# A projection in two sweeps: queries and gate of the retention computed chunk by chunk

## The reference, cut to what matters

```python
h  = rmsnorm(x, g_norm_mix) * (1.0 + sc1) + sh1          # [2048, 1024]
hc = rmsnorm(ctx, g_norm_mix) * (1.0 + csc1) + csh1      # [256, 1024]
cq, ckv, kr, rq, rk, rv, rg = split(h @ w_in, (256, 128, 32, 512, 512, 512, 512))   # the same for hc
q_a, k_a, v_a = mla_qkv(cq, ckv, kr, ...)                # rmsnorm, @ w_uq, @ w_ukv, 2-D rope
q, k = rope_2d(rq), rope_2d(rk * 64 ** -0.5)             # 8 heads of 64; gate = rg
# per direction (decay gamma_h), per chunk n of 128 tokens:
s       = (q_n @ k_n.T) * decay_in
u_n     = (k_n * zeta).T @ v_n
r_{n+1} = decay_chunk * r_n + u_n                        # starts from the context's state
y_n     = s @ v_n + (q_n * xi) @ r_n
# out: y normed per head, * g_ret, * silu(rg); concatenated with attention; @ w_o
```

## Time and profile before

| | us |
|---|---|
| median of 3 runs (lowest, highest) | 3234.02 (3233.12, 3239.76) |
| the profiled execution | 3241.32 |
| its span in the trace | 3239.5 |
| `modulation` | 0 to 124.6 |
| `project` | 124.6 to 897.8 |
| `retention` | 897.8 to 1103.9 |
| `attention`, `mix_out`, `experts` and final output | 1103.9 to 3239.5 |

### The profile page before, as it was taken

One profiled execution on the slowest core, in us unless ns is written; L12 is line 12 of the kernel. 1 busy time (PEld: TensorE's weight loads), 2 busy tenths in 40 slices (PEclk: granted clock), 3 DMA queues, 4 the chain that ended last, 5 costly groups with the idle time before them and its releaser, 6 DMA issues. The chain is left out here.

```text
span 3239.5 us, 55402 instructions
## 1 busy us (share of the span) xinstructions
PE 2990.5 (92%) x20325; PEld 2205.0 (68%) x20325; DVE 2014.4 (62%) x2973; ACT 1381.0 (43%) x2069; POOL 353.2 (11%) x385
## 2 busy tenths in 40 slices
PE   6799999999978699999999998899399999999997
PEld 1355555555578667666666665787398989899996
DVE  1133333333357599989899998445766666666766
ACT  0133333333222377677677765211244444444444
POOL 0011111111145200000000000221001111010102
PEclk9899999999977699999999999999599999999998
DMA  8511111111132301110111000533467676666768
GB/s 313 176 65 64 64 60 61 61 64 64 52 111 78 82 3 34 37 25 14 35 27 25 23 6 12 179 135 113 137 205 209 206 222 208 201 203 211 212 202 312
DMA packets 255042, 365.51 MB, mean 113 GB/s; under 512 B 36469, under 2 KB 170616, under 8 KB 253177
## 3 DMA queue, kind: packets, MB, share of 16 engines
q1 hardware_dynamic: 245336, 327.97, 31.5%
q0 software_dynamic: 9504, 34.61, 4.5%
HBM read 280.70 MB, written 81.83 MB: 112 GB/s over the span
## 5 line engine op out<-in xcount | busy, mean ns | idle before, releaser
L479 PE MATMUL bank<-w_in_sb,h_T 128*128 128x512 f32 (+1 forms) x1440 | 609.9, 578 | 2.1 <-DVE h_T L628 2.1
L1784 PE MATMUL ebank<-gathered_T,w_gate_up 128*128 128x256 f32 x4608 | 561.2, 284 | 21.8 <-issue 16.4
L1784 PEld LDWEIGHTS ebank<-gathered_T,w_gate_up 128*128 128x128 f32 x4608 | 556.7, 193 | 25.6 <-issue 20.7
L479 PEld LDWEIGHTS bank<-w_in_sb,h_T 128*128 128x128 f32 x1440 | 270.4, 191 | 299.4 <-issue 299.1
L1062 PE MATMUL abank<-head_qT,head_kT 96*128 96x512 f32 x1728 | 414.7, 400 | 23.2 <-DVE head_qT L1171 17.0
L1062 PEld LDWEIGHTS abank<-head_qT,head_kT 96*128 96x128 f32 x1728 | 326.3, 192 | 104.6 <-issue 29.6
L1142 ACT ACTIVATE scores<-scores 128x1536 f32<-128x1536 f32 x192 | 274.3, 1476 | 232.8 <-DVE scores L1201 232.8
L1201 DVE TENSOR_TENSOR scores<-scores,abank 128x1536 f32<-128x1536 f32 x192 | 322.7, 1748 | 44.9 <-PE abank L1082 44.8
L1137 ACT ACTIVATE scores<-abank 128x512 f32<-128x512 f32 x576 | 325.7, 602 | 42.5 <-PE abank L1062 17.1
L1092 PE MATMUL abank<-scores,head_v 128*64 128x256 f32 x2304 | 291.0, 388 | 1.2 <-ACT scores L1142 1.2
L1798 PE MATMUL ebank<-w_down,hidden_T 128*128 128x512 f32 x1152 | 282.0, 400 | 2.9 <-DVE w_down L2016 2.8
(11 more groups left out here) (266 smaller groups left out, 3291.8 us busy)
## 6 DMA issues: line engine op xcount, KB each, us to landing
w_gate_up_whole<-in_w_exp_gate SPq DMA_DIRECT2D x48, 1024.0 KB, 5.7
w_gate_up_whole<-in_w_exp_up SPq DMA_DIRECT2D x48, 1024.0 KB, 9.0
w_down_whole<-in_w_exp_down SPq DMA_DIRECT2D x192, 256.0 KB, 6.0
ada_w<-in_w_ada SPq DMA_DIRECT2D x12, 2048.0 KB
scratch_ret<-ret_rows SPq DMA_DIRECT2D x72, 256.0 KB, 2.5
x_tile<-in_x_all SPq DMA_DIRECT2D x18, 512.0 KB
w_in_sb<-in_w_in SPq DMA_DIRECT2D x4, 2048.0 KB, 18.2
chunk_qk<-scratch_ret SPq DMA_DIRECT2D x16, 512.0 KB
```

What stands on the lines that cost most here:

```text
L479: m = pe.matmul(banks[bank][:, 0:n], hT[u][:, k, :], w_in[:, k, lo:lo + n], start=(k == 0), stop=(k == KD - 1))
L1784: x = pe.matmul(banks[f % 3][:, j * CAP:(j + 1) * CAP], w_gu[c][:, wp, j, k, o:o + P], xsT[:, xp, k, :], start=(k == 0 and n == 0), stop=( ...
```

## The change

The projection's w_in is split into a rounded part and a rest, and so is h_T; the products take three fp32r matmuls per k-tile. The first sweep, `project`, computes only the latent, rk and rv. It stores the modulated h_T of each tile, and the state of each chunk, to DRAM. The attention's queries are left out for the context's two tiles. The products of a tile's turn are interleaved anew: two, transposes of the next x, transposes of the latent, the third product. h's rest is taken on VectorE at the end of its turn and waits for the store of h, since it overwrites it. The weights for rq and rg (4 MB) are loaded meanwhile.

The second sweep, `retention`, loads h_T, rk, rv and the states. At its start it splits the weights for rq and rg in 16 pieces. Per chunk TensorE makes both products of the next chunk back to back, then the scores, output transposes, transposes of the next chunk, outputs and the decayed transposes. VectorE ropes rq, decays the scores and after that computes the gate; the rest of h closes its turn. The scores and the transposed q_xi keep one buffer instead of two and share banks 4 and 5.

`modulation` gets three ScalarE copies and three VectorE subtractions that split w_in.

```diff
@@ modulation
+            for part, c in enumerate(IN_PARTS):                                   # ACT, after the decays
+                act.wait_ge(w_loaded[1 + part], 16)
+                act.activation(weights["in"][:, 0, :, c], weights["in_whole"][:, 1, :, c], ACT.Copy).then_inc(s_w_in, 1)
...
+                if 5 <= n < 8:                                                      # DVE
+                    c = IN_PARTS[n - 5]
+                    dve.wait_ge(s_w_in, n - 4)
+                    dve.tensor_tensor(weights["in"][:, 1, :, c], ..., ALU.subtract).then_inc(w_rest, 1)
@@ project, SP
+                store(t, "ret_k", rk[:, :], scratch["rk"][at, :], "rk_stored")
+                if ahead:
+                    store(t + 1, "hT", hT_whole[1 - u][:, 1, :, :], scratch["h"][bass.ds(row + P, P)], "h_stored")
...
+                store(t, "u_back", st[u][:, :], scratch["state"][at, :], "state_stored")
@@ project, TensorE
+            def z(t, u, bank, lo, n):
                 for k in range(KD):
+                    for i, (hp, wp) in enumerate(((0, 0), (0, 1), (1, 0))):
+                        m = pe.matmul(banks[bank][:, 0:n], hT[u][:, hp, k, :], w_in[:, wp, k, lo:lo + n],
+                                      start=(k == 0 and i == 0), stop=(k == KD - 1 and i == 2))
...
+                sg["h_rest"].wait(pe, t)
+                z(t, u, 0, 0, LAT)
+                z(t, u, 1, LAT, RW)
+                if ahead:
+                    xT(pe, t + 1, 1 - u)
                 sg["kr_lat"].wait(pe, t)
...
+                z(t, u, 3, LAT + RW, RW)
                 sg["latT"].wait(pe, t)
+                if queries:
...
-                z(u, 0, LAT + 2 * RW, RW)
-                z(u, 3, LAT + 3 * RW, RW)
@@ project, VectorE
+            def rest(t, u):
+                sg["h_stored"].wait(dve, t)
+                for g in range(2):
+                    k = slice(4 * g, 4 * g + 4)
+                    sg["h_rounded"].wait(dve, t, g + 1)
+                    dve.tensor_tensor(hT[u][:, 1, k, :], hT_whole[u][:, 1, k, :], hT[u][:, 0, k, :].bitcast(F32), ALU.subtract).then_inc(sg["h_rest"].sem, 1)
...
+                if ahead:
+                    x_norm(t + 1, 1 - u)
+                if not (isinstance(t, int) and t == 0):
+                    advance_state(t - 1, 1 - u)
...                                     # latent normed, rope of rk
+                if ahead:
+                    modulate(t + 1, 1 - u)
...                                     # latent_T scaled
+                if ahead:
+                    rest(t + 1, 1 - u)
@@ retention, TensorE
             def turn(r, u, first, ahead):
-                if ahead >= 1:
-                    scores(r + 1)
-                outputs(r, u)
-                if ahead >= 2:
-                    transposes(r + 2, u)
+                if ahead:
+                    z_query(r + 1, 1 - u)           # waits h_rest(r + 1), ret_q(r)
+                    z_gate(r + 1, 1 - u)            # waits gate(r)
+                scores(r)
                 if not first:
                     out_transposes(r - 1)
+                if ahead:
+                    transposes(r + 1, 1 - u)
+                outputs(r, u)
+                if ahead:
+                    decayed_transposes(r + 1)
@@ retention, VectorE
+            def turn(r, u, first, ahead):
+                if not first:
+                    out_rows(r - 1)
+                if ahead:
+                    rope_q(r + 1, 1 - u)
+                if ahead:
+                    next_carry(r + 1, 1 - u)
+                decay_scores(r)
+                if ahead:
+                    gate_rows(r + 1)
+                if ahead == 2:
+                    rest_h(r + 2, u)
@@ retention, ScalarE
+            def turn(r, u, first, ahead):
+                evacuate_kq(r)
+                if not first:
+                    square(r - 1)
+                evacuate_qx(r)
+                if ahead:
+                    gate_exp(r + 1)
                 if not first:
                     store(r - 1)
+                if ahead == 2:
+                    round_h(r + 2, u)
@@ retention, GpSimd
+                if not first:
+                    power_of(r - 1)
+                pool.tensor_tensor(gg[:, :], gate[:, :], gret[:, :], ALU.mult).then_inc(sg["gate_gain"].sem, 1)
+                if ahead:
+                    q_xi(r + 1)
```

More of the change, by code:

```diff
@@ L469, in xT @@
             m.then_inc(sg["xT_psum"].sem, 1)
-            sg["k_rows"].wait(pe, t - 1)
+            if not (isinstance(t, int) and t < 2):
+                sg["k_rows"].wait(pe, t - 2)
             for k in range(4):
@@ L544, in x_stats, with round_h, turn @@
                 act.activation(xst[:, 1:2], xst[:, 1:2], ACT.Exp, scale=-0.5).then_inc(sg["x_rstd"].sem, 1)
-            def turn(t, u, ahead):
+            def round_h(t, u):
+                sg["z_psum"].wait(act, t - 2)
+                for g in range(2):
+                    k = slice(4 * g, 4 * g + 4)
+                    sg["hT"].wait(act, t, 2 * g + 2)
+                    act.activation(hT[u][:, 0, k, :], hT_whole[u][:, 1, k, :], ACT.Copy).then_inc(sg["h_rounded"].sem, 1)
+            def turn(t, u, ahead, queries):
+                if ahead:
+                    x_stats(t + 1, 1 - u)
                 sg["z_psum"].wait(act, t, 1)
@@ L590, in _, with turn @@
         def _(pool):
-            def turn(t, u, ahead):
-                sg["q_rows"].wait(pool, t)
+            def turn(t, u, ahead, queries):
+                sg["ret_k"].wait(pool, t)
+                sg["u_psum"].wait(pool, t - 1)
+                for w in range(2):
+                    pool.tensor_tensor(kz[:, :, w, :], halves(rk[:, :]), last(perm["zeta"][:, w * H:(w + 1) * H], 64), ALU.mult).then_inc(sg["k_zeta"].sem, 1)
+                if not queries:
+                    return
+                n = t - TC
                 tables.wait(pool, t, u)
+                sg["q_rows"].wait(pool, n)
                 x = q_sb[:, :, NOPE:]
@@ L756, in _ @@
+            top = (T - 1) * P
+            load_h(top, 0)
+            load_back(P, 0)
+            sp.dma_start(back[1][b, :], scratch["state"][64:128, :]).then_inc(context_loaded, 16)
+            load_k(top, 0)
+            load_v(top, 0)
+            load_h(top - P, 1)
+            load_k(top - P, 1)
+            load_v(top - P, 1)
             sp.dma_start(gret[:, :], ins["g_ret"].partition_broadcast(P)).then_inc(gret_loaded, 16)
[L757 to L759 removed]
@@ L801, in _, with z @@
+            q_xi(0)
             loop(pool, turn)
+            power_of(TM - 1)
         @block.tensor
         def _(pe):
+            def z(r, u, bank, part, first):
+                for k in range(KD):
+                    if first:
+                        pe.wait_ge(w_rest, part * KD + k + 1)
+                    for i, (hp, wp) in enumerate(((0, w_hi), (0, w_lo), (1, w_hi))):
+                        m = pe.matmul(banks[bank][:, :], hT[u][:, hp, k, :], wp[:, k, part * RW:(part + 1) * RW],
+                                      start=(k == 0 and i == 0), stop=(k == KD - 1 and i == 2))
+                m.then_inc(sg["z_psum"].sem, 1)
@@ L805, in transposes, with z_query, z_gate @@
+            def z_query(r, u, first=False):
+                sg["h_rest"].wait(pe, r)
+                sg["ret_q"].wait(pe, r - 1)
+                z(r, u, 0, 0, first)
+            def z_gate(r, u, first=False):
+                sg["gate"].wait(pe, r - 1)
+                z(r, u, 1, 1, first)
             def transposes(r, u):
-                kq_loaded.wait(pe, r, u)
+                kb_loaded.wait(pe, r, u)
                 sg["chunk_kqT"].wait(pe, r - 1)
-                for b, which in ((0, 1), (1, 0)):
+                sg["ret_q"].wait(pe, r)
+                for bank, x in ((2, rk[u]), (3, rq)):
@@ L927, in turn, with out_rows @@
+            def out_rows(r):
                 sg["y_psum"].wait(dve, r)
```

536 lines of the change are left out of this document (307 added, 229 removed).

## The result

The changed kernel takes 3059.93 us (median of 4 runs, 3048.09 to 3068.14), the kernel before 3235.74 in 4 runs on the same chip: a ratio of 0.9453, with an interval of 0.9419 to 0.9486. The forecast was 3070 with a range of 3040 to 3140, and faster. The profiled execution of the changed kernel took 3068.14 us, with a span of 3066.3.

A forecast was written before the change was run, and what follows sets the result against it. TensorE alone was taken to bound the projection, while the retention ran at a mean clock of 0.72. First sweep -295.4 us and second +131.0 gave -164.4, so 3076.9 profiled and 3070 as median, range 3040 to 3140.

The forecast's parts named there:

- The product: Both sweeps: 24 fp32r matmuls of 512 columns take 5.55 us instead of 6.87 in plain f32.
- Rival E: Both sweeps: fp32r products as dear as f32 records, 408 us more, 3478; chance 0.01.
- The latent tile: First sweep: 25.0 us for each of 16 latent tiles, set by the chain through latent_T; bounds 23.9 and 28.
- collision: First sweep: modulation sums on VectorE beside GpSimd's k_zeta cost 1.32 us instead of 0.69; one or two hit.
- The context tiles: First sweep: 21.7 us for each of two tiles without queries, set by the store of h, above TensorE's 20.5.
- The chunk: Second sweep: 19.7 us a chunk, a loop closing through VectorE's rest of h; bounds 18.6 (TensorE) and 25.
- The fill: Start of the second sweep: loading h, rounding, splitting weights, rope and q_xi; first turn starts at 23.8 us.
- The end: End of the second sweep: last out_rows, decay, outputs, transposes, copy and barrier take 19.0 us.
- The price of the gate in front: Second sweep: with the gate before the decay, outputs wait until 18.3 and a chunk costs 4 us more.
- rival A: Second sweep keeps falling to the lower clock: 25.1 us a chunk, 81 us more, 3150; chance 0.13.
- B: First sweep: late h store or VectorE collisions make the turn 27.5 us instead of 25.0, 3110; chance 0.18.
- C: Fewer collisions: 24.0 us a turn in the first sweep, 18.8 in the second, 3041; chance 0.09.

The follow-up runs named there:

- late_latent: Changed kernel plus one VectorE row sum of 0.69 us just before it scales latent_T in the first sweep; 3076.87 us, one run.
- rest_first: Changed kernel with h's rest taken before the gate on VectorE in the second sweep, and that h rounded earlier on ScalarE; 3042.27 us, ratio 0.9382.
- no_reciprocal: Changed kernel with the gate's reciprocal left out in the second sweep; 3041.23 us, one run.
- gate_first: Changed kernel with VectorE computing the next chunk's gate before it decays the scores in the second sweep; 3173.76 us, ratio 0.9793.
- gate_first_busy: gate_first plus 14 fp32r products of constant operands on TensorE before the outputs of each chunk, result unread; 3120.99 us, one run.
- the two comparisons: Changed kernel against the kernel before, run twice: 3059.93 us, ratio 0.9453; again, unaltered, 3052.96 us, ratio 0.9424.

## Why the prediction was right, point by point

**What bounds the kernel, and where.** Right for both sweeps: in the steady stretches the only recorded waits of TensorE are those named.

**The product.** 5.55 us was taken from the output stage's 24 matmuls. Measured in the second sweep: (757.13 - 745.95)/2 = 5.59. What follows latent_T took 6.96 (357.81 to 364.77) for a forecast of 6.95. Rival E is out.

**The latent tile.** 25.0 predicted, 24.33 measured (389.2/16, with the shorter last one; 24.39 without it). The mechanism was right, late_latent shows it, and a term was mis-sized. The prediction had latent_T ready 18.1 us after the start of product 0; in the tile shown it was 17.4 (340.28 to 357.68). The steps one by one: 5.25 to z_latent (5.1), 5.8 to the last roped row (5.94), 2.1 for the rope (2.0), 3.2 for the modulation (353.43 to 356.63) where 2.74 and a collision of 0.9 to 1.0 were taken, 1.05 for the scaling (1.04). The collision cost 0.46, since just one of the two sums was hit for long; the other 0.3 are tenths added at handovers, which were in the durations already. The same tenths are in the 17.3 at which TensorE was said to want latent_T. The third product starts at 11.4 to 11.5 and takes 5.55, which gives 17.0, and only this agrees with the prediction's sum of 23.96 (17.0 + 6.95). So the chain is late by some 0.4, where the prediction took 0.8.

What the collision does can be read from the rows. The sum at 354.24 began 0.48 us before k_zeta's first multiplication ended (353.67 + 1.05) and took 0.33 more than alone. The second multiplication began at 354.67, while that sum ran to 355.26, and took 0.45 more. The sum at 355.99 met only the last 0.17 of it and took 0.03 more. Each loss is no longer than what was left of the other engine's instruction. The Trainium skill (SBUF — State Buffer, "SBUF: two separate sides") has the shared port as an exclusive lock that is kept for the whole instruction. The prediction made of this a wait of a whole 1.04; what follows from it is a wait for the rest of the instruction that is under way, and with that the rows here agree.

**The context tiles and the ends.** By the third tile's first product the run was 3.9 us ahead of the forecast (193.93 instead of 197.8): the first product came at 151.5 (152.0), and a context turn took 20.7 and not 21.7. Here a step failed. The prediction had the store of h set that turn, with 3.1 us from issue to landing. In the trace VectorE did wait for the store in the first two turns (1.83 and 1.85 us), but the rest of h was ready at 172.68 and the products started at 173.29, right behind TensorE's own last step and without a wait. TensorE's work set the turn (20.5 by the prediction's sum). The tail was 4.9 (5.5). With 9.9 from the 16 latent tiles this is the first sweep's whole difference: 588.0 instead of 602.4.

**The chunk.** 19.7 predicted, 19.44 measured in the turn shown (19.39 in the mean), and with the same steps: products 11.18 (11.1), decay done at 13.7 (13.7), gate done at 18.2 (18.3), rest at 19.3 (19.6). That this is a loop through the rest of h is shown by rest_first, and the second bound, TensorE's 18.6, by the 18.52 there and by no_reciprocal. The fill was 22.2 (23.8). The end was dearer than its 19.0: from the last transposes at 900.2 to 922.0 it took 21.8, with the clock at the lower level from 905 on (a granted clock of 0.50). The stage took 334.0 (337.1).

**The price of the gate in front.** Here the prediction failed: "the chunk would cost 4 us more" in this order; it costs 7.2, as gate_first shows (7.6 in a full turn). The wait was nearly right (3.5 to 3.7), but it takes the place of the 0.9 us by which the loop was above TensorE's work, so at full clock the turn grows by just 2.95. The step that was missing is that a wait of this length costs the clock of what follows: 4.4 of the 7.2 by gate_first_busy. The prediction had this mechanism as rival A, but asked it only of the order that the change has. Of the parts of the change that were tried here, decay ahead of the gate is worth the most: 113 us of stage against the order with the gate first.

**Rival A.** Not what the change does: 1.00 in both steady stretches, 0.95 in the mean of the stage, which has a start and an end at the lower clock. The Trainium skill (TensorE: Matmul & The Clock Gate, "Part 4: PE-mode transpose") says that transposes do not count as activity as matmuls do. In this kernel 7.5 us of transposes, scores and 64-column matmuls stand in each turn and the clock holds, and it falls when a wait of 3.5 us is added in the same stretch. So this work alone did not make it fall. Whether it would have held through the gap with other work around is not shown, and no run has transposes alone.

**Rivals B and C.** C (24.0 and 18.8, 3041) was nearer for the first sweep (24.39) and the forecast for the second (19.39 against 19.7). B's 27.5 did not come; late_latent shows that a further step in that chain is paid in full.

**The sum.** -164.4 predicted, -181.9 in the trace at the start of attention: of the difference of 17.5, 14.4 are from the first sweep and 3.1 from the second. All terms were a little too dear but the second sweep's end, which was too cheap by 2.8. The medians give -175.8 and -186.8 in the two comparisons. That the first of them lies so near is in part luck: in the profiled executions the unchanged stages from attention on took 8.7 us longer after the change (2144.3 against 2135.6), which hides half of the error in the sweeps.

## What to carry to other kernels

When work is moved between stages, cost each new turn as a loop: start at one engine's first step, follow it to the handover that lets that step start again, and only then compare it with each engine's sum of work; here the loop (19.4) and TensorE (18.5) were 0.9 us apart, and one reordering (rest_first) took just that. On the engine that closes the loop, put first what TensorE waits for, and price a wait on TensorE in its own time and in the clock behind it (here, 3.5 us of wait were followed by 8 us at a mean of 0.59). A cheaper instruction is worth its full difference only up to the next chain: in the first sweep the 3.65 us of three cheaper products (2 x 1.32 and 1.01 by the prediction's prices) brought 3.25 (27.17 - 23.92), and the missing 0.4 is what TensorE now stands for latent_T.

## What the runs showed of the hardware that was not expected

- A gap of 3.5 us on TensorE, in the middle of turns at full clock, was followed by 8 us at a mean clock of 0.59; with the gap filled by constant products the clock stayed at 1.00 and the stage was 68.5 us shorter.
- VectorE and GpSimd side by side on SBUF delay each other, each by no more than what was left of the other's instruction: a sum of two 128x512 tensors took 0.72 to 1.02 us instead of 0.69, a multiplication of the carried state 1.42 instead of 0.69, and GpSimd's pair for q_xi 3.00 instead of 2.08. The one that began first of two was not slowed: the carried state's sum at 754.07 took 0.69 with q_xi behind it from 754.11.
- A reciprocal of 128x512 in float32 takes VectorE 3.35 us, where a sum of the same size takes 0.69: it was VectorE's largest single step in the second sweep's loop.
